# Attention layers: where the mix norm's lower half is summed, rooted, scaled and turned

## The reference

```python
for i in range(DEPTH):
    h = rmsnorm(x, attn_norm[i])
    proj = h @ w_in[i]
    qa, ka, va, qb, kb, vb = jnp.split(proj, IN_SPLITS, axis=-1)
    ...
    oa = dilated_mixer(qa, ka, heads(va, N_HEADS_A))
    ...
    ob, _ = banded_attention(qb, kb, heads(vb, N_KV_B), SWA_WINDOW - 1,
                             sink=sinks[i].reshape(N_KV_B, GQA_GROUP))
    ...
    mix = jnp.concatenate([rmsnorm(merge_heads(oa), mix_norm_a[i]),
                           rmsnorm(merge_heads(ob), mix_norm_b[i])], axis=-1)
    x = x + mix @ w_out[i]
```

## Time and profile before

| what | us |
| --- | --- |
| median of 3 runs | 2677.37 |
| the three runs | 2671.5, 2677.37, 2678.55 |
| the profiled execution | 2677.7 |
| its span in the trace | 2675.9 |
| TensorE busy in it | 2551.6 (95%) |
| VectorE busy | 1824.0 (68%) |
| ScalarE busy | 1452.0 (54%) |

### The profile page before, as it was taken

How to read it: one execution, slowest core, us unless ns; L and a number is a source line. 1 busy time by engine, 2 the same in 40 slices (tenths; PEclk the granted TensorE clock), 3 DMA queues, 4 the chain that set the end, 5 groups by cost and what they waited for, 6 DMA issues and landing times.

```text
span 2675.9 us, 33561 instructions
## 1 busy us (share of the span) xinstructions
PE 2551.6 (95%) x11949; PEld 2028.0 (76%) x11949; DVE 1824.0 (68%) x1779; ACT 1452.0 (54%) x1613; POOL 57.5 (2%) x40
## 2 busy tenths in 40 slices
PE   7899998888999999999999998999999999998998
PEld 6578887666878787888888886888884687776787
DVE  6554555559898989888888886555443475776544
ACT  4554434545777777777777675445432343465443
POOL 0000000016000000000000000000000000000000
PEclk9989998889999999999999998999999999999999
DMA  6865542758999999999999996556543344435552
GB/s 216 294 215 186 184 169 79 252 181 328 356 348 349 353 342 358 348 351 349 353 340 361 332 345 217 180 182 194 181 166 108 99 148 119 137 100 175 195 185 70
DMA packets 327742, 631.65 MB, mean 236 GB/s; under 512 B 14088, under 2 KB 112936, under 8 KB 327464
## 3 DMA queue, kind: packets, MB, share of 16 engines
q1 hardware_dynamic: 326792, 627.35, 67.5%
q0 software_dynamic: 864, 3.15, 0.3%
HBM read 629.40 MB, written 1.05 MB: 236 GB/s over the span
## 4 chain that ended last, share of the span: by engine, by line
PE 84%; DVE 8%; ACT 4%; issue 3%; DMA 1%; SPq 0%; DVEq 0%; ACTq 0%
PE ps L894 18%; PE ps L820 18%; PE ps L924 11%; PE ps L849 9%; PE ps L1289 6%; PE ps L754 5%; PE ps L1316 2%; PE ps L1221 2%; DVE As L2261 2%; PE ps L1027 1%; PE ps L949 1%; ACT As L1679 1%; PE ps L833 1%; PE ps L909 1%; PE ps L1280 1%
## 5 line engine op out<-in xcount | busy, mean ns | idle before, releaser
L2261 DVE TENSOR_TENSOR As<-ringA,As 128x2048 fp32r<-128x2048 f32 x318 | 737.8, 2322 | 220.2 <-ACT As L1598 127.5
L894 PE MATMUL ps<-As,xgs 128*128 128x512 f32 x2688 | 660.9, 395 | 10.5 <-DVE As L2261 7.8
L894 PEld LDWEIGHTS ps<-As,xgs 128*128 128x128 f32 x2688 | 494.9, 188 | 117.6 <-DVE As L2261 6.8
L1679 ACT ACTIVATE As<-ringA 128x2048 fp32r<-128x2048 f32 x224 | 428.7, 1914 | 29.9 <-PE ps L894 28.1
L820 PE MATMUL ps<-As,xs 128*128 128x512 f32 x1632 | 391.5, 396 | 9.3 <-DVE xs L2199 5.3
L820 PEld LDWEIGHTS ps<-As,xs 128*128 128x128 f32 x1632 | 305.8, 189 | 76.1 <-issue 5.7
L924 PE MATMUL ps<-Bs,hds 128*128 128x512 f32 x1332 | 324.6, 393 | 13.7 <-DVE hds L2322 13.5
L924 PEld LDWEIGHTS ps<-Bs,hds 128*128 128x128 f32 x1332 | 250.0, 189 | 72.5 <-issue 19.3
L2341 DVE TENSOR_TENSOR Bs<-ringB,Bs 128x2048 fp32r<-128x2048 f32 x111 | 260.4, 2346 | 11.0 <-ACT Bs L1709 9.5
L1709 ACT ACTIVATE Bs<-ringB 128x2048 fp32r<-128x2048 f32 x111 | 213.1, 1920 | 74.8 <-PE ps L924 74.8
L849 PE MATMUL ps<-Bs,hds 128*128 128x512 f32 x1056 | 247.8, 390 | 0.0
(11 more groups left out here) (380 smaller groups left out, 3210.2 us busy)
## 6 DMA issues: line engine op xcount, KB each, us to landing
ringA<-in_moe_w_gate SPq DMA_DIRECT2D x112, 1024.0 KB, 5.1
ringA<-in_moe_w_up SPq DMA_DIRECT2D x112, 1024.0 KB, 5.7
ringB<-in_moe_w_down SPq DMA_DIRECT2D x112, 1024.0 KB, 5.5
ringA<-in_w_ff_in SPq DMA_DIRECT2D x132, 512.0 KB, 4.8
ringA<-in_w_in SPq DMA_DIRECT2D x56, 1024.0 KB, 5.4
ringA<-in_w_ada SPq DMA_DIRECT2D x36, 1024.0 KB, 6.2
ringB<-in_w_ff_out SPq DMA_DIRECT2D x33, 1024.0 KB, 5.0
ringA<-in_dense_w_gate SPq DMA_DIRECT2D x28, 512.0 KB, 3.6
```

Source lines behind the costliest of these rows:

```text
L894: m = mm(ps[:, bank, :], lhs(l, tt, k), As[:, h, r, k % 4, :], start=k == 0 and n == 0, stop=k == KC - 1 and n == 2)
L1679: A(As[:, h, 0, :, :], ringA[:, (p["a"] + u) % 2, 4 * h:4 * h + 4, :], ACT.Copy).then_inc(A_high, 1)
L2261: V.tensor_tensor(As[:, h, 1, :, :], ringA[:, (p["a"] + u) % 2, 4 * h:4 * h + 4, :], f32(As[:, h, 0, :, :]), ALU.subtract).then_inc(A_spli ...
```

## The change

Three engines' programs are changed, for both layers.

ScalarE: the lower half's `tile_stats` move to the middle of group 2, behind its copies and ahead of `mods(6)` and the exponentials of group 3. Its `tile_root` moves behind group 3's copies. The root's table is loaded by an instruction of its own, behind the first of those copies. Of the first column block's weights, half 0 is split before the upper half's statistics and half 1 after `spreads(8)`. The upper half's statistics now stand ahead of the copy of `mods(8)`, and the lower half's `rows_high` behind the upper root.

TensorE: `values(3)` and `mods(8)` come ahead of the lower half's turn; `spreads(8)` stays behind it.

VectorE: the lower half's `tile_scale` moves from behind `outputs(2)` to behind `weights(3)` with its copies, and its `rows_low` from there to behind the upper half's `tile_scale`.

```diff
@@ TensorE, heads @@
                     if g == 3:
+                        values(g)
+                        mods(8)
                         pe.wait_ge(nm_ready, 4 * (l + 1))
                         for tt in range(TILES):
                             turn_rows(f"mix{l}", tt, 0)
-                        values(g)
-                        mods(8)
                         spreads(8)
                         continue
@@ ScalarE @@
                         A(PT[:, j, :], ps[:, 2, 0:384], ACT.Copy).then_inc(pt_act, 1)
                         if j == 0:
+                            if g == 3:
+                                nc.scalar.preload_act_table(ACT.Sqrt)
                             spreads(2 * g + 1)
+                    if g == 2:
+                        for tt in range(TILES):
+                            tile_stats(f"mix{l}", tt, O, [(o_done, 4 * l + 2)], slice(0, D // 2), tt)
                     if g < 3:
                         mods(2 * g + 2)
                         exponentials(g + 1, (0, 1))
                         spreads(2 * g + 2)
                         exponentials(g + 1, (2, 3))
                         mods(2 * g + 3)
-                    if g == 2:
-                        for tt in range(TILES):
-                            tile_stats(f"mix{l}", tt, O, [(o_done, 4 * l + 2)], slice(0, D // 2), tt)
-                        tile_root(0, 2, D // 2)
+                tile_root(0, 2, D // 2)
...
+                weight_high(p, 0, 0)
+                for tt in range(TILES):
+                    tile_stats(mix, tt, O, [(o_done, 4 * (l + 1))], slice(D // 2, D), 2 + tt)
+                mods(8)
+                tile_root(2, 4, D // 2)
                 for tt in range(TILES):
                     rows_high(mix, tt, 0, mixc)
-                for h in range(2):
-                    weight_high(p, 0, h)
-                mods(8)
-                for tt in range(TILES):
-                    tile_stats(mix, tt, O, [(o_done, 4 * (l + 1))], slice(D // 2, D), 2 + tt)
-                tile_root(2, 4, D // 2)
                 spreads(8)
+                weight_high(p, 0, 1)
                 for tt in range(TILES):
                     rows_high(mix, tt, 1, mixc)
@@ VectorE @@
                     if g == 3:
                         for tt in range(TILES):
-                            rows_low(mix, tt, 0, mixc)
+                            tile_scale(mix, tt, O, 1, lower, tt)
                     outputs(g)
-                    if g == 2:
-                        for tt in range(TILES):
-                            tile_scale(mix, tt, O, 1, lower, tt)
                 weight_low(p, 0, 0)
                 for tt in range(TILES):
                     tile_scale(mix, tt, O, 2, upper, 2 + tt)
+                for tt in range(TILES):
+                    rows_low(mix, tt, 0, mixc)
                 weight_low(p, 0, 1)
```

## The result

The changed kernel takes 2658.3 us in the median of 13 runs (2654.04 to 2673.92). The kernel before, run beside it, takes 2678.55 (2669.09 to 2687.35, 13 runs). The ratio is 0.9935, with a 95% interval of 0.9915 to 0.9955, so the change gains 17 us (12 to 23). That ratio is formed over all the runs; the two medians by themselves are 20.3 us apart, and I go by the ratio. Forecast were 2661.7 us in a range of 2655 to 2670.

A forecast was written before the change was run, and what follows sets the result against it. TensorE, 95% busy, was held up in group 3 by waits for ScalarE's and VectorE's copies and, at larger cost, by the low clock. Layer 0's 8.1 plus layer 1's 7.9 us off 2677.7 gave 2661.7, range 2655 to 2670.

The forecast's parts named there:

- The statistics at no cost: ScalarE, group 2: two moved statistics, 1.48 us, fit an idle 1.66 us; otherwise group 3's exponentials up to 1.5 us late.
- Copies and values, layer 0: Group 3, layer 0: values start near 125.7 and not 131.42, take 2.72 us, and the table's load is hidden.
- The chain of ScalarE and VectorE: Layer 0, from w_out's landing at 128.6 to the projection's upper products at 140.5; mark 8.8 us earlier before clock allowance.
- The clock in layer 0: Projection, layer 0: a clock falling in waits between 131 and 135 may reach past 140.5; 0.7 us allowed, leaving 8.1.
- The clock in layer 1: Group 3, layer 1: clock back about a microsecond after the turns, 7.9 us gained; 3.9 if low until the projection.
- The mark: Layer 0: issue of the next stage's first load, 154.91 before; layer 1: end of the projection's 60th product, 559.77 before.
- The sum: Both layers: 8.1 + 7.9 = 16.0 us off the profiled execution's 2677.7, giving 2661.7.
- The clock low in one layer: First rival: clock stays low from group 3 to the projection in one layer; 12.0 us gained, 2665.7; chance 0.18.
- The gain taken back by new waits: Second rival: upper products wait on eight steps of two engines and, in layer 0, a landing; 2671.7; chance 0.10.
- The repeated load: Third rival: copies need the old table, so two more loads in each layer cost 5.1 us; 2666.8; chance 0.03.
- Slower through a low clock in the projection: Fourth rival: low clock through the projection's 96 products, 20.4 us a layer; 2702.5; chance 0.05 with other failures.
- The rule on transposes: Skill's rule: full clock does not engage for transposes; layer 1's turns would not restore it, 3.9 us in place of 7.9.

The follow-up runs named there:

- stats_twice: The changed kernel with the lower half's two statistics done twice in group 2; 2658.37 us, one run.
- tile_again: A second run of the changed kernel with both row tiles' lower-half products first in the output projection's first column block; 2650.54 us, ratio 0.9903.
- tile_order: The changed kernel with both row tiles' lower-half products first in the output projection's first column block; 2654.68 us, ratio 0.9899.
- no_preload: The changed kernel without the instruction that loads the root's table early, so the load comes with the root; 2673.21 us, one run.

## Why the prediction was right, point by point

**The statistics at no cost.** Right: 0.35 us are left ahead of `arow` in layer 0, and 1.26 in layer 1.

**Copies and values, layer 0.** Right. The values begin 123.10 - 120.71 = 2.4 us behind the first turn; forecast were 125.7 - 123.04 = 2.7. They take 2.72 as said, and the load of the table is hidden.

**The chain of ScalarE and VectorE.** Right in each step: from the landing to the 13th product it takes 137.75 - 126.23 = 11.5 us, where the sum had 140.5 - 128.6 = 11.9. The landing was at 6.2 us after the issue, as before. This is what makes the new wait of TensorE, released by VectorE's `rows_low` as said.

**The clock in layer 0.** It fell behind the first of the new waits, at 131.7, as feared, and was back before the 13th product. So it cost nothing where I allowed 0.7: 9.0 and not 8.1 us.

**The clock in layer 1.** It fell as the turns began, and returned with them. The mark came 29.35 us after group 3's first turn; 551.2 + 0.7 - 523.07 = 28.8 were forecast. The step that was too small is the allowance of 0.7 for the clock in the projection: the clock fell again behind the wait of 1.96 (at 527.8), and the 48 products there took 12.94 us where 11.3 were counted, so 1.6. Hence 7.2 us and not 7.9.

**The sum.** 16.2 us in the two stretches; 16.0 forecast. The runs say 17 (12 to 23). That the sum comes so near is in part luck: layer 0 gained 0.9 more than forecast and layer 1 0.7 less. So is how near the median of 2658.3 came: it is 3.4 below the forecast, and one execution's total moves by more than that with the clock.

**The rivals.** The clock low in one layer was real, as a chance of each execution. After the same fall at the turns of layer 1's group 3 it returned in the changed kernel, its repetition, `stats_twice` and `tile_again`, and not until the modulation block was nearly done in `tile_order` and `no_preload`. TensorE's timeline of `tile_again`, against that of `tile_order` above:

```profile
511.68 3.15 PE L1082 MATMUL ps<-c,arena 128*128 128x128 f32 x12 [0.72 <-ACT small L1857]
...
517.59 1.92 PE L1042 MATMUL ps<-ringA,cT 128*32 128x512 f32 x16
```

I gave the return as what is expected, from one row. It is the more frequent case, with a price near 3 us when it fails (`no_preload`, 32.2 against 29.3). The gain taken back by new waits: in part, 0.82 and 1.96 us, both counted ahead of time. The repeated load: no, one load per layer in this part. Slower through a low clock in the projection: no; in every profiled execution it came back within it, where it fell at all.

**The rule on transposes.** The best case is layer 1 of the kernel before. The clock fell there at 513.1 and was back at 516.5. The last of the values ended at 513.8, the modulation block began at 516.71, and between them TensorE did nothing but turns. Read in windows of 0.2 us, the granted clock is 0.50 from 513.1 on, still 0.50 from 516.3 to 516.5, and 0.96 from 516.5 to 516.7.

In layer 1 of the changed kernel TensorE did twelve turns without a wait from 510.47 and the first values from 513.33, and the clock was back at 514.0. By the rule of the Trainium skill ("TensorE: Matmul & The Clock Gate", "Part 4: PE-mode transpose") the turns should not have counted. The trace disagrees with that as I had applied it: the low clock through the values, which I took to follow from the rule, didn't come. But in the six executions in which the clock fell there and no wait followed, it returned so early in four only. And some value products ran beside the turns in both cases, so it is not shown that turns alone would do.

## What to carry to other kernels

Price a stall of the matmul engine by what runs behind it at the lower clock, and not by its own length: here two waits, 2.4 us in layer 0 and 2.2 in layer 1, cost 1.2 us by themselves and 9.3 through the clock, which they brought down or kept down. Test it with idle products in the wait, which needs three lines and separates the two. When a chain of other engines has become the bound, look for products that are ready while TensorE waits for those that are not.

## What the runs showed of the hardware that I had not expected

Idle products whose result nobody reads made the kernel before as fast as the reordered one within the intervals (0.9936 and 0.9931), with the granted clock at 1.00 through a window that read 0.70 before.

The clock also falls where TensorE has not waited. In layer 1 of the kernel before it reads busy for all of each microsecond from 503 to 513, and yet the clock fell at 513.1. What ran last there were small products: eight of 2 columns at 509.85 and then values of 64 columns. So a filled timeline is not yet a high clock.

And the total of one and the same kernel is spread: the 13 runs of the changed kernel lie between 2654.04 and 2673.92 us, which is more than the gain, at mean granted clocks from 0.985 down to 0.977. Its two stretches agreed within 0.1 us in its two profiled executions, but those of `tile_order` and `tile_again`, one kernel too, are 2.9 us apart in layer 1.
